# Query, key and value stage: heads turned two tiles behind, latents two tiles ahead, weights loaded one stage earlier

## What is computed

```python
u = _rmsnorm(h, attn_norm_w[l])
proj = u @ w_in[l]
q_lat, kv_lat, k_pe = proj[..., :c1], proj[..., c1:c2], proj[..., c2:c3]
...
q = (_rmsnorm(q_lat, q_a_norm_w) @ w_q_b).reshape(B, L, MLA_HEADS, QK_HEAD_DIM)
kv = (_rmsnorm(kv_lat, kv_a_norm_w) @ w_kv_b).reshape(B, L, MLA_HEADS, QK_NOPE_DIM + V_HEAD_DIM)
k_nope, v = kv[..., :QK_NOPE_DIM], kv[..., QK_NOPE_DIM:]
k = jnp.concatenate([k_nope, jnp.broadcast_to(k_pe[:, :, None, :], (B, L, MLA_HEADS, QK_ROPE_DIM))], axis=-1)
q = _rmsnorm(q, q_norm_w)
k = _rmsnorm(k, k_norm_w)
q = jnp.concatenate([q[..., :QK_NOPE_DIM], _rope(q[..., QK_NOPE_DIM:], pos)], axis=-1)
k = jnp.concatenate([k[..., :QK_NOPE_DIM], _rope(k[..., QK_NOPE_DIM:], pos)], axis=-1)
```

## Time and profile before

| | us |
|---|---|
| median of 3 runs | 3298.81 |
| lowest, highest | 3288.57, 3303.06 |
| profiled execution | 3297.44 |
| its span in the trace | 3295.7 |

### The profile page before, as it was taken

The page is one execution under the profiler, slowest core; times in us unless marked ns, Lnnn a source line. Parts: engine busy times, 40 slices in busy tenths (PEclk is TensorE's granted clock), DMA queues, the critical chain, the costliest instruction groups (busy, mean ns, idle before and its releaser), DMA issues. The chain is left out here.

```text
span 3295.7 us, 49545 instructions
## 1 busy us (share of the span) xinstructions
PE 2888.7 (88%) x19127; PEld 2511.9 (76%) x19127; DVE 1815.8 (55%) x2751; ACT 1186.7 (36%) x2196; POOL 1100.0 (33%) x1195
## 2 busy tenths in 40 slices
PE   6995655999499979999399869999999999699999
PEld 6994545999488868888277658888878888588887
DVE  3214541443255557777489656566697777534444
ACT  3223531222244445554243333333343333323312
POOL 2602440000676710000245235555566666200000
PEclk9997877999699989999699979999999999899999
DMA  6953446322434331220346543223343333545454
GB/s 232 376 163 92 118 108 246 104 61 81 104 96 100 70 91 55 70 76 23 112 152 215 175 161 96 90 90 96 96 159 114 104 109 96 177 140 189 164 170 147
DMA packets 413459, 421.85 MB, mean 128 GB/s; under 512 B 38282, under 2 KB 335766, under 8 KB 412214
## 3 DMA queue, kind: packets, MB, share of 16 engines
q1 hardware_dynamic: 370558, 302.18, 30.2%
q10 hardware_dynamic: 30360, 71.82, 6.7%
q0 software_dynamic: 12320, 44.80, 4.1%
HBM read 258.18 MB, written 160.55 MB: 127 GB/s over the span
## 5 line engine op out<-in xcount | busy, mean ns | idle before, releaser
L2791 PE MATMUL fu_pM<-fu_us_hi,fu_w_hi 128*128 128x512 f32 x1232 | 489.8, 398 | 35.1 <-DVE fu_us_lo L2624 35.1
L2791 PE MATMUL fu_pM<-fu_us_lo,fu_w_hi 128*128 128x512 f32 x1232 | 486.6, 395 | 0.0
L2791 PE MATMUL fu_pM<-fu_us_hi,fu_w_lo 128*128 128x512 f32 x1232 | 486.2, 395 | 0.0
L2791 PEld LDWEIGHTS fu_pM<-fu_us_hi,fu_w_hi 128*128 128x128 f32 x1232 | 236.2, 192 | 87.4 <-issue 28.6
L2791 PEld LDWEIGHTS fu_pM<-fu_us_hi,fu_w_lo 128*128 128x128 f32 x1232 | 235.6, 191 | 50.2
L2791 PEld LDWEIGHTS fu_pM<-fu_us_lo,fu_w_hi 128*128 128x128 f32 x1232 | 236.3, 192 | 49.0
L3026 PE MATMUL fd_pM<-fd_bs_hi,fd_a_hi 128*128 128x512 f32 x616 | 242.1, 393 | 26.7 <-DVE fd_bs_lo L2958 22.6
L3026 PE MATMUL fd_pM<-fd_bs_hi,fd_a_lo 128*128 128x512 f32 x616 | 241.2, 391 | 0.0
L3026 PE MATMUL fd_pM<-fd_bs_lo,fd_a_hi 128*128 128x512 f32 x616 | 240.8, 391 | 0.0
L2538 ACT ACTIVATE fu_w_hi<-fu_sw 128x512 fp32r<-128x512 f32 x176 | 111.0, 631 | 324.7 <-PE fu_pM L2791 262.7
L2953 DVE TENSOR_TENSOR fd_a_lo<-fd_a_lo,fd_a_hi 128x1408 fp32r<-128x1408 f32 x56 | 91.0, 1625 | 237.6 <-ACT fd_a_hi L2909 237.6
(11 more groups left out here) (403 smaller groups left out, 7195.6 us busy)
## 6 DMA issues: line engine op xcount, KB each, us to landing
fd_a_lo<-scr_gs ACTq DMA_DIRECT2D x56, 704.0 KB, 4.5
fu_w_raw<-in_w_gate SPq DMA_DIRECT2D x22, 1024.0 KB, 5.2
fu_w_raw<-in_w_up SPq DMA_DIRECT2D x22, 1024.0 KB, 5.2
scr_gs<-fu_sg SPq DMA_DIRECT2D x88, 256.0 KB, 2.7
scr_gs<-fu_acc SPq DMA_DIRECT2D x66, 256.0 KB, 2.5
pj_wd<-in_w_down POOLq DMA_DIRECT2D x11, 1024.0 KB, 11.2
scr_td<-pj_td POOLq DMA_DIRECT2D x11, 1024.0 KB, 8.9
fd_b_raw<-scr_td SPq DMA_DIRECT2D x44, 256.0 KB, 4.9
```

The source lines that it names most:

```text
L2791: p = pe.matmul(bank(2 * n + m, i)[:, :], a[:, k, :], x[:, k, :], start=(k == 0 and n_pass == 0), stop=(k == HALVES_K - 1 and n_pass == 2))
```

## The change

- The qkv stage's weights and six vectors are no longer loaded at its start. Their buffers (`qw_raw`, `qw_lat_gain`, ...) are allocated around both stages, and SP asks for them in the project stage, at step 6 (`load_next`), eight transfers. `build` therefore wraps the first two stages in one more cleanup.
- The weights are split in two parts on ACT and DVE; the products of the queries wait for the first, those of keys and values for the second.
- Offsets: PE transposes the latents of t+2 (before t+1) and makes the final transposes of t-2 (before t-1). ACT and DVE follow: latents of t+3, `l_hi` and `l_lo` of t+2, out of t-2. SP loads t+4 and stores t-2.
- On ACT the `l_hi` copy stands between the evictions and the squares, and out before the roots. The store of the values goes from ACT's queue to SP's. On DVE `qn` comes before `kn`; `kx` is in two parts, the first waiting for PE alone (before: for ACT's `qx`). On POOL the key's products come before the wait for `qn`. `kpe` has four buffers, and its sum of squares its own four.
- All loops of the stage are written out (`plain`).

```diff
+            def load_next(t, s, u):
+                if t == 6:
+                    for of, name in ((slice(0, QW), "w_q_b"), (slice(QW, QW + KVW), "w_kv_b")):
+                        sp.dma_start(S["qw_raw"][:, :, of], A[name][0].rearrange("(k p) n -> p k n", p=P)).then_inc(S["qw_loaded"], 16)
...
-            plain(TILES, (2, lambda t, s, u: load(t, s, u) if t >= 2 else None), (0, store), (-1, store_tok))
+            plain(TILES, (2, lambda t, s, u: load(t, s, u) if t >= 2 else None), (0, store), (-1, store_tok), (0, load_next))
...
-            steps(sp, TILES, (3, load), (1, load_tables), (-1, store))
+            plain(TILES, (4, load), (0, store_values), (-2, store), (1, load_tables))
...
-            tiles(pool, TILES, None, rotate)
+            pool.wait_ge(S["q_consts"], 96)
+            plain(TILES, (0, rotate))
...
-            steps(act, TILES, (1, latents_hi), (0, heads), (0, head_roots), (2, latents), (-1, out))
+            plain(TILES, (0, heads), (2, latents_hi), (0, squares), (-2, out), (0, roots), (3, latents))
...
-                dve.tensor_tensor(kn[s][:, :, :], kv[s][:, :, 0:NOPE],
-                                  hs[s][:, 2, 4:8].unsqueeze(2).to_broadcast([P, HEADS, NOPE]), ALU.mult)
+                if u:
+                    dve.wait_ge(turned[s], u)
                 dve.tensor_tensor(qn[s][:, :, :], q[s][:, :, :],
                                   hs[s][:, 2, 0:4].unsqueeze(2).to_broadcast([P, HEADS, QK]),
                                   ALU.mult).then_inc(scaled[s], 1)
+                dve.tensor_tensor(kn[s][:, :, :], kv[s][:, :, 0:NOPE],
+                                  hs[s][:, 2, 4:8].unsqueeze(2).to_broadcast([P, HEADS, NOPE]), ALU.mult).then_inc(k_scaled[s], 1)
...
-            steps(dve, TILES, (1, latents_lo), (1, rotary_key), (0, heads), (0, scale), (2, latents), (-1, out))
+            plain(TILES, (2, latents_lo), (-2, out_nope), (0, heads), (-2, out_rope), (1, rotary_key), (0, scale), (3, latents))
...
             def out(t, s, u):
+                pe.wait_ge(k_scaled[s], u + 1)
                 pe.wait_ge(q_rotated[s], u + 1)
                 pe.wait_ge(k_rotated[s], u + 1)
-                pe.wait_ge(kx_ready[1 - s], u + s)
+                if t:
+                    pe.wait_ge(kx_ready[1 - s], u + s)
...
-            steps(pe, TILES, (0, heads), (1, latents), (-1, out))
+            plain(TILES, (0, heads), (2, latents), (-2, out))
...
+    with nc.cleanup_on_exit(), ExitStack() as ctx:
...
+        run(stage_project, stage_qkv)
+    run(stage_conv, stage_delta, stage_attention, stage_out, stage_gate_up, stage_down)
```

More of the change, by code:

```diff
@@ L408, in _ @@
         def _(sp):
[L409 to L416, removed]
@@ L468, in rotate @@
                 pool.wait_ge(trig_loaded[s], 16 * (u + 1))
+                pool.wait_ge(kg_ready, t + 1)
                 for m, (part, table) in enumerate(((0, cos), (1, sin), (0, sin), (1, cos))):
[L470 to L472 removed]
@@ L473, in rotate @@
-                pool.wait_ge(pool_step, per * t + n[0])
-                pool.wait_ge(k_rotated[s], u)
+                    pool.tensor_tensor(kprod[:, m, :], kg[s][:, part * HALF:(part + 1) * HALF], table, ALU.mult).then_inc(k_prod, 1)
+                pool.wait_ge(k_prod, 4 * t + 4)
+                if t:
+                    pool.wait_ge(k_rotated[1 - s], u + s)
                 pool.tensor_tensor(kturn[:, 0:HALF], kprod[:, 0, :], kprod[:, 1, :], ALU.subtract)
                 pool.tensor_tensor(kturn[:, HALF:], kprod[:, 2, :], kprod[:, 3, :], ALU.add).then_inc(k_turned[s], 1)
-                pool.wait_ge(turned[s], u)
+                pool.wait_ge(scaled[s], u + 1)
@@ new lines, in rotate @@
+                pool.tensor_tensor(qg[:, :, :], qn[s][:, :, NOPE:], rope_gain[:, 0:1, :].to_broadcast([P, HEADS, ROPE]),
+                                   ALU.mult).then_inc(q_gained, 1)
+                pool.wait_ge(q_gained, t + 1)
+                for m, (part, table) in enumerate(((0, cos4), (1, sin4), (0, sin4), (1, cos4))):
+                    pool.tensor_tensor(qprod[:, m, :, :], qg[:, :, part * HALF:(part + 1) * HALF], table,
+                                       ALU.mult).then_inc(q_prod, 1)
@@ L522, in heads, with squares @@
-                act.activation(junk_k[:, :, :], kv[s][:, :, 0:NOPE], ACT.Square).then_inc(squares[s], 1)
-            def head_roots(t, s, u):
+            def squares(t, s, u):
+                act.wait_ge(q_out[s], u + 1)
+                if t:
+                    act.wait_ge(sums[1 - s], u + s)
+                act.activation(junk[:, :], q[s][:, :, :].rearrange("p h d -> p (h d)"), ACT.Square)
+                act.wait_ge(kv_out[s], u + 1)
+                act.activation(junk_k[:, :, :], kv[s][:, :, 0:NOPE], ACT.Square).then_inc(squares_made[s], 1)
@@ L3031, in build, with run @@
 def build(nc, A, S, only=None):
-    for name, stage in STAGES:
-        if only is None or name in only:
+    def run(*stages):
+        for stage in stages:
             with nc.cleanup_on_exit():
                 stage(nc, A, S)
-STAGES = [("project", stage_project), ("qkv", stage_qkv), ("conv", stage_conv), ("delta", stage_delta), ("attention", stage_attention),
-          ("out", stage_out), ("gate_up", stage_gate_up), ("down", stage_down)]
+    with nc.cleanup_on_exit(), ExitStack() as ctx:
+        r = Room(nc, ctx, "qw")
+        S["qw_raw"], S["q_lat_gain"] = r.sb("raw", [P, 2, QW + KVW]), r.sb("lat_gain", [P, 2 * LORA])
+        S["q_nope_gain"], S["q_rope_gain"] = r.sb("nope_gain", [P, 2]), r.sb("rope_gain", [P, 2, ROPE])
+        S["qw_loaded"], S["q_consts"] = r.sem("loaded"), r.sem("consts")
+        run(stage_project, stage_qkv)
+    run(stage_conv, stage_delta, stage_attention, stage_out, stage_gate_up, stage_down)
 SCRATCH = {
```

192 lines of the change are left out of this document (113 added, 79 removed).

## The result

The changed kernel takes **3250.94 us** (median of 4 executions, 3247.38 to 3256.48), the kernel before 3299.97 beside it (4 executions): a ratio of **0.9857**, 95% interval 0.9840 to 0.9873. The forecast was 3241, its range 3224 to 3262. Its terms missed on both sides: the qkv stage won more than I had said, and the projection stage lost far more.

The account below looks back on a forecast made before the run. The steady qkv stretch was taken as bound by a chain across engines, 11.53 us a tile. Loop 51.4 + front 6.3 + tail 3.8 - projection 5.0 - cleanup 0.5 = 56.0 off 3297.4 gave 3241 us, range 3224 to 3262.

Parts of the forecast that it names:

- The turn two tiles behind: Qkv loop: the lap of some 22 us carries three tiles instead of two, 7.3 us a tile, and stops being the bound.
- The latents' round trip: Qkv loop: DVE's scaled latents, PE's transposes, ACT's `l_hi`, then DVE's `l_lo`; sets the time, DVE idle about 1.4 us a tile.
- T = 8.5: Qkv loop: time per steady tile, 8.5 us with `kn` slowed by POOL, 8.2 without; ends 7.7 and 9.6.
- The loop, +51.4: Qkv stage, first product of tile 0 to that of tile 16: 133.2 us instead of 184.56, saving 51.4 us.
- The front, +6.3: Start of the qkv stage: weights already in SBUF, first product at about 271.3 instead of 277.65, saving 6.3 us (4 to 8).
- The tail +3.8: Qkv stage, tile 16's first product to the next stage: 29.84 us before, saving 3.8 us (2 to 5).
- the cleanup -0.5: After the qkv stage: one more semaphore clear and barrier, costing 0.5 us (0 to 0.9).
- The projection, -5.0: Projection stage: the early weight loads delay x loads while DMA is full and stall PE, costing 5.0 us (0 to 10).
- Rival 3: Projection stage: weight loads hold SP's queue 10 us or more and PE cools, another 8 us, 3249 us; chance 0.08.
- Rivals 2, 4 and 5: Qkv loop: clock pays for gaps, 3255 us (0.12); SP becomes the bound, 3256 (0.04); PE stays at lower level, 3313 (0.02).
- Rival 5: Qkv loop: PE stays at its lower level, 3313 us, slower than before from about 12.1 us a tile; chance 0.02.
- Rival 1: Qkv loop: no contention between POOL and DVE, full clock, 7.7 us a tile, 3232 us; chance 0.12.

Follow-up runs that it names:

- the reordered kernel: The changed kernel with the latents on DVE put ahead of kg, qn and kn, and ACT's part a tile further ahead: 3237.1 us (0.9813).

## Why the prediction was right, and where it was not

- *The turn two tiles behind stops the lap from being the bound*: right. POOL is waited for by nobody, and the run with one tile of lag gives the whole gain back.
- *The latents' round trip is late next, with DVE idle 1.38 us before `l_lo`*: right to 0.01 us, and the reordered kernel cuts it to 0.70 in the step shown. PE idles 1.27 us a tile, where I had 1.7 to 1.9.
- *T = 8.5*: mis-sized, 8.15. The layout from rows alone had given 8.2. The 0.3 I added were for `kn`, which I let stretch under POOL as `latn` does. It kept its 0.69, which I had named as a sign of being wrong; POOL's `qg` paid instead, 1.11 for 0.74, in POOL's 2.1 us of slack. I had taken the scaled latents' row for a rule about another operation, and had not asked which of the two starts first. The GPSIMD Engine Reference of the Trainium skill, section 1, Specifications, says that the two engines contend when VectorE's instruction has two SBUF inputs. Both pairs do here (`latn` 0.88 without `qg`, 1.35 and 1.56 beside it; `qg` 1.11 beside `kn`). It doesn't say who pays, so "by that rule `kn` pays" was my addition.
- *The loop, +51.4*: from 292.63 to 422.48 are 129.85 us, so 184.56 - 129.85 = 54.7. The first steps came at 7.3, 8.9 and 9.5, near the layout (7.4, 8.4, 9.1).
- *The front, +6.3*: 17.70 - 10.61 = 7.1. The run with the loads at the head confirms what it consists of.
- *The tail +3.8 and the cleanup -0.5*: 29.84 - 27.77 = 2.1 in all instead of 3.3. Of the cleanup little can be seen: from the end of SP's last issue to the next stage are 3.10 us (447.15 to 450.25) for 2.99 in before.
- *The projection, -5.0, between 0 and -10*: the step that failed. It measured -14.5 (-22.1 in the profiled pair). The form was right: a full DMA period, the x load late, PE waiting for `u_lo`. The size was mis-set: the 1.84 MB of the two weight loads alone, where all eight are 2.17 MB, at the rate of all queues (373 GB/s), less 0.63 us of cover. The traces show POOL's traffic keeping its share, so that SP's rate is what counts: 17.76 MB in 105 us, by which 1.84 MB are 10.8 us and all 2.17 MB 12.8 (estimates). The runs show the weights at 7.0 and the six small loads, which I had priced at nothing, at 4.3, each give or take 2.7. I had named the case that POOL keeps its share, but as the outer end, -10, without a row. And the delay can't drain: PE is busy without a gap behind the full period.
- *Rival 3*, the projection paying 8 us more, is what came true, beside a loop 3.3 us and a front 0.8 us better: by the profiled pair 54.7 + 7.1 + 2.1 - 22.1 = 41.8, by the means of the executions 63.9 - 14.5 = 49.4, where the two medians differ by 49.0. I had given it 0.08. *Rivals 2, 4 and 5* asked for a clock or a queue that fails in the loop; clock 0.97, and no engine waits for SP's stores. Rival 5's turning point of 12.1 us a tile left the projection's cost out; the run with one tile of lag shows no gain at 11.2. *Rival 1* had `latn` at 0.88, which the reordered kernel shows (0.89), but not in this order.
- *The time*, 10 us over the forecast and within its range: the projection cost 9.5 us more than forecast, the qkv stage brought some 3 more, and the kernel before ran 2.6 us over the execution I had summed against (3299.97 for 3297.4). That the misses partly cancel is luck.
- The Trainium skill's sentence that all issuing engines share the same 16 DMA engines (DMA: Bandwidth & Descriptors, section Issuing engines are not separate DMA queues) agrees with the runs: moved to ACT's queue, the loads still cost 9.2 us (standard error 2.4) of the 14.5.

## What to carry over

Look at the DMA share of the stretch that a prefetch is moved into: the same eight loads cost 14.5 us in a period at 1.0 and nothing that shows eight tiles later. Moving them within the queue did not help, and most of the cost stayed on another one. Price them at the rate of the queues that give way (here SP's, 169 GB/s), not at that of all. When a lag takes away one chain, lay the next step out from rows; the wait that appears then names the next reorder, here another 11 us. And before a difference of ten microseconds is read from one pair of traces, look how far traces of the same code lie apart.

## What I had not expected of the hardware

- The projection stage without the early loads ended between 259.4 and 269.3 us in five traces. From the start of the stage behind qkv to the end (the profiled execution's time less that start), unchanged code took 2797.5 to 2813.0 us over all traces.
- An issue on SP's queue took up to 12.4 us in the full period (`scr_tok`, the run with only the weights early) and up to 11.4 in a kernel without early loads, against mostly 0.3 to 0.7 behind it.
- Contention between POOL and DVE had no fixed payer. `kn`, starting first, cost `qg` 0.4 us and kept its 0.69; `latn`, starting behind `qg`, grew by 0.47 and by 0.68 us, and `qg` kept its 0.72 where only `latn` ran beside it. In the reordered kernel `latn` runs beside POOL's `kprod` instead and mostly keeps its 0.88, while the four `kprod` take 1.1 to 1.3 us, where they take 0.90 in the changed kernel.
